# An encoder's forward pass on one core: the SBUF buffers placed in another order, the large ones at multiples of 512 bytes

## The reference

```python
def reference(x, mem, diff_w_qkv, ..., ctx_2, ada_w_2, ssd_w_in_2, ..., ffn_w_out_2):
    x = first_block(x, mem, ...)       # differential attention, dilated attention;
                                       # after each: cross-attention to mem, conv GLU network
    return second_block(x, c_2, ctx_2, ...)   # adaptive norms; an SSD mixer (context, then
                                              # latent), a conformer convolution, two SwiGLU

def memory_cross_attention(x, mem, w_q, w_kv, w_o):
    q = (x @ w_q).reshape(B, S, H, E)
    kv = (mem @ w_kv).reshape(B, M, 2, H, E)
    s = jnp.einsum('bshe,bmhe->bhsm', q, kv[:, :, 0]) * (E ** -0.5)
    o = jnp.einsum('bhsm,bmhe->bshe', softmax(s), kv[:, :, 1])
    return o.reshape(B, S, D) @ w_o

def swiglu(h, w_in, w_out):
    u = h @ w_in
    return (jax.nn.silu(u[..., :FFN_HIDDEN]) * u[..., FFN_HIDDEN:]) @ w_out
```

## Time and profile before

| | us |
|---|---|
| median of 3 runs | 2053.28 |
| lowest, highest | 2052.96, 2055.01 |
| the profiled execution | 2055.43 |
| its span, first to last instruction | 2053.7 |

### The profile page before, as it was taken

The page is one execution under the profiler, slowest core; times in us unless marked ns, Lnnn a source line. Parts: engine busy times, 40 slices in busy tenths (PEclk is TensorE's granted clock), DMA queues, the critical chain, the costliest instruction groups (busy, mean ns, idle before and its releaser), DMA issues.

```text
span 2053.7 us, 34088 instructions
## 1 busy us (share of the span) xinstructions
PE 1920.8 (94%) x13629; PEld 1700.4 (83%) x13629; DVE 1109.8 (54%) x1524; ACT 998.6 (49%) x1726; POOL 1252.0 (61%) x585
## 2 busy tenths in 40 slices
PE   7989999999999989989999899898789999999997
PEld 7879799887999866868888788876579988968996
DVE  5472346623700172146667655678728962847981
ACT  4654345543444373435543444377845545525542
POOL 8768467686888405456778344300369886417995
PEclk9999999999999999999999899999999999999999
DMA  7435377774555405357764122211245554324552
GB/s 259 144 129 203 120 269 308 303 264 167 185 186 185 143 1 183 146 218 299 313 257 146 64 81 86 99 64 62 82 154 184 184 185 147 120 82 159 195 187 104
DMA packets 49217, 342.30 MB, mean 167 GB/s; under 512 B 5264, under 2 KB 7312, under 8 KB 8144
## 3 DMA queue, kind: packets, MB, share of 16 engines
q1 hardware_dynamic: 47440, 331.02, 44.1%
q0 software_dynamic: 1664, 9.70, 1.2%
HBM read 339.65 MB, written 1.05 MB: 166 GB/s over the span
## 4 chain that ended last, share of the span: by engine, by line
PE 77%; DVE 11%; ACT 6%; POOL 3%; issue 2%; DMA 1%; DVEq 0%; SPq 0%; ACTq 0%; POOLq 0%
PE bank L1708 13%; PE bank L1712 13%; PE bank L1763 13%; PE bank L1710 12%; PE bank L1813 3%; PE bank L1743 2%; PE bank L1742 2%; PE bank L1740 2%; PE bank L1939 2%; PE bank L1309 2%; PE bank L1311 2%; PE bank L1312 2%; ACT arena L1140 2%; DVE arena L723 2%; PE bank L1531 1%
## 5 line engine op out<-in xcount | busy, mean ns | idle before, releaser
L2219 POOL TENSOR_TENSOR w_lo<-ring,w_hi 128x1024 fp32r<-128x1024 f32 x360 | 877.0, 2465 | 275.2 <-ACT w_hi L2827 258.0
L1708 PE MATMUL bank<-x_hi,w_hi 128*128 128x256 f32 x2176 | 618.5, 284 | 18.6 <-POOL w_lo L2219 14.1
L1712 PE MATMUL bank<-x_lo,w_hi 128*128 128x256 f32 x2176 | 619.7, 285 | 0.0
L2827 ACT ACTIVATE w_hi<-ring 128x1024 fp32r<-128x1024 f32 x448 | 448.9, 1052 | 332.8 <-DMA ring<-slabs_dram 326.1
L1708 PEld LDWEIGHTS bank<-x_hi,w_hi 128*128 128x128 f32 x2176 | 415.8, 191 | 38.5 <-issue 37.3
L1712 PEld LDWEIGHTS bank<-x_lo,w_hi 128*128 128x128 f32 x2176 | 415.0, 191 | 0.0
L1710 PE MATMUL bank<-x_hi,w_lo 128*128 128x256 f32 x1472 | 414.3, 281 | 0.0
L1710 PEld LDWEIGHTS bank<-x_hi,w_lo 128*128 128x128 f32 x1472 | 282.4, 192 | 0.0
L2219 POOL TENSOR_TENSOR w_hi<-ring,w_hi 128x1024 fp32r<-128x1024 f32 x88 | 208.8, 2394 | 102.7 <-ACT w_hi L2827 102.7
L2751 ACT ACTIVATE arena<-bank 128x512 f32<-128x512 f32 (+1 forms) x178 | 97.9, 563 | 279.6 <-PE bank L1712 192.1
L1710 PE MATMUL bank<-x_hi,w_hi 128*128 128x256 f32 x704 | 197.5, 281 | 0.0
(11 more groups left out here) (355 smaller groups left out, 3665.1 us busy)
## 6 DMA issues: line engine op xcount, KB each, us to landing
ring<-slabs_dram SPq DMA_DIRECT2D x308, 1024.0 KB, 4.8
lnrow<-ln_dram POOLq DMA_DIRECT2D x6, 1024.0 KB, 5.3
arena<-slabs_dram SPq DMA_DIRECT2D x4, 1024.0 KB, 8.3
xt<-xT_dram SPq DMA_DIRECT2D x1, 1024.0 KB, 5.9
xt<-memT_dram SPq DMA_DIRECT2D x1, 1024.0 KB, 12.0
x<-x_dram SPq DMA_DIRECT2D x1, 1024.0 KB, 13.6
arena<-ctx_dram POOLq DMA_DIRECT2D x1, 1024.0 KB, 8.0
lnrow<-ln_dram POOLq DMA_DIRECT2D x2, 512.0 KB, 5.0
```

The lines of the kernel that those rows point to most:

```text
L1708: ins = pe.matmul(dst, wh[:, k, c], src[0][:, k, :], start=(k == 0), stop=False)
L1712: ins = pe.matmul(dst, wh[:, k, c], src[1][:, k, :], start=False, stop=(k == KC - 1))
L2219: pool.tensor_tensor(dst[:, c], ring[:, s, c], w_hi[:, s, c].bitcast(F32), ALU.subtract).then_inc(S["lo_ready"], 1)
L2827: a.activation(w_hi[:, g % RING, c], ring[:, g % RING, c], ACT.Copy) \
```

## The change

Only the order of the allocations changes. `row` and `mod` (2176 and 768 bytes) go to the front; `pt`, `small` and `sc_in` (3264, 2304 and 1024 bytes) go behind the arena. All instructions, their order and their waits stay; their SBUF addresses are others.

```diff
+        row = sb("row", [P, NROW])
+        mod = sb("mod", [P, 2, 6, 8, 2])
         ring_at = aligned()
         ring = sb("ring", [P, RING, SLAB])
         x = sb("x", [P, NT, D])
...
         tri_at = aligned()
         tri = sb("tri", [P, 4, NT, T])
         lnrow = sb("lnrow", [P, 2, D])
-        pt = sb("pt", [P, NPT])
-        row = sb("row", [P, NROW])
-        small = sb("small", [P, 576])
-        mod = sb("mod", [P, 2, 6, 8, 2])
-        sc_in = sb("sc_in", [P, KC, 32])
         xlat = sb("xlat", [P, KC, T])
         arena_at = aligned()
         arena = sb("arena", [P, 28672])
+        pt = sb("pt", [P, NPT])
+        small = sb("small", [P, 576])
+        sc_in = sb("sc_in", [P, KC, 32])
```

## The result

| | before | after |
|---|---|---|
| median, us | 2053.57 (4 runs) | 2068.86 (4 runs) |
| lowest, highest | 2052.96, 2055.01 | 2066.51, 2069.48 |
| span of the profiled execution | 2053.7 | 2067.8 |

The changed kernel is slower by 15.3 us between the medians (0.74%); the ratio on record, from the single runs, is 1.0069, 95% interval 1.0056 to 1.0081. The forecast was 2080.8 us, with a range that began at 2070.0.

What follows compares the result with a forecast made beforehand. The prediction took PE's rate between matmul starts as the bound. Its terms summed to 29.4 us, 28.0 at the granted clock, +27.5 after 0.5 off, so 2053.3 + 27.5 = 2080.8 us, range 2070 to 2088.

Steps and rivals of the forecast that it cites:

- What bounds the kernel: Whole span: PE is busy 94%, waits offer little, so only PE's rate from one matmul to the next matters.
- The 256-column terms: x columns rise to 360 ns a triple, 19.6 us; conv networks, m columns and L1740 on m, 6.4 us.
- Half clock: All PE terms: at 1.2 GHz, 4.6% of the time, places cost nothing, so 29.4 us becomes 28.0.
- The 512-column term: L1763 and L1531: two more equal pairs in each group of six matmuls, 3.4 us slower; L1309 unchanged.
- last sign: If PE's spacing is as forecast but the span isn't 20 us longer, something assumed on the path was not.
- Rival B: Faster, about 2020 us: buffers off a 512-byte mark cost, so at 0 every pair gets the cheapest price; 4%.
- Plain fp32: fp32 matmuls such as L1813 run at half the rate and don't depend on places: 0 us.
- Transfers at 0: DMA into the ring lands at 0 instead of 128: taken as 0 us, with -5.5 to +4.3 considered.
- Rival A: Nothing changes, 2053.3 us: PE's two streams don't disturb each other and the levels come from something else; 7%.
- Rival C: Half the effect, 2067 to 2070 us: only pairs equal in more than the low nine bits cost fully; 2%.
- Rival D: Over 2088 us: triples with every pair equal at 0 also meet GpSimd's and ScalarE's reads there; 3%.
- A count of pairs: fp32r triples: each pair of moving operand and next weights at equal addresses modulo 512 costs 6.7 ns.

Runs made afterwards that it cites:

- tri alone: Against the kernel before: only tri (x_lo) and lnrow at 128 modulo 512, every other large buffer at 448; 2052.54 us, ratio 0.9988.
- both at 128: Against the kernel before: xlat and the arena moved to 128 modulo 512, where the ring and its neighbours already began; 2066.89 us, ratio 1.0068.
- ring alone: Against the kernel before: only the ring (w_lo) at 128 modulo 512, everything else large at 448; 2064.48 us, ratio 1.0051.
- 32, 96 and 128 bytes of distance: Three layouts against the kernel before: ring group at 128, arena and xlat at 160, 480 or 0 modulo 512; 2059.74, 2074.74 and 2057.0 us.
- x_hi apart: Against the kernel before: tri at 128, other large buffers at 448 modulo 512, x_hi and x_lo exchanged so x_hi lies in tri; 2059.63 us, ratio 1.0025.
- the ring at 0 and the arena at 448: Against the kernel before: ring and its neighbours moved to 0 modulo 512, xlat and the arena staying at 448; 2059.25 us, ratio 1.0024.
- x_hi apart and the others at 320: Against the kernel before: x_hi in tri at 128, row moved behind the arena, other large buffers at 320 modulo 512; 2060.0 us, ratio 1.0025.

## Why the prediction was wrong in size, point by point

**What bounds the kernel: right.** PE's busy time and the span grew by 14.9 and 14.1 us, its longest wait by nothing. The granted clock is unchanged. In the stretch of the earlier trace rows PE is now never idle, and GpSimd is 12.5 us below it, where it was 10.0 below before (busy us of PE, its loads, VectorE, ScalarE, GpSimd; clock, DMA share):

```profile
1545.00:1665.00 120.00, 120.00 (x1002) 120.00 (x1002) 103.43 (x60) 59.33 (x83) 107.49 (x44) 1.00 0.49 179
```

**The 256-column terms: right.** Forecast 360.0 ns for every form, measured 359.5 to 360.0. The terms of 19.6 and 6.4 us came to 25.4 together, by the table. The rule that gave them, 6.7 ns for each equal pair, is not right: it fails in six of the layouts above. What carried the terms is its upper end, which was measured at 360 (L1740 on x, L1309). That these mixed-place forms have in the mean the same 360 as a form with everything at one place is luck as far as these runs tell; at 512 columns the same step from one to the other failed.

**Half clock: right.** The prediction left the share of time at 1.2 GHz out. At half clock a triple of x columns takes 640 ns before and after, which is one column a cycle (3.2 us over five triples, and 3.9 over six to the tenth of a us, 640 by the starts to the ns; first the kernel before, then the changed one):

```profile
L1708 PE MATMUL bank<-x_hi,w_hi x6: 415/415/416, 501.2 to 504.4; 128*128 128x256 f32 x6
...
L1708 PE MATMUL bank<-x_hi,w_hi x7: 415/415/415, 505.0 to 508.9; 128*128 128x256 f32 x7
```

**The 512-column term: the step that failed.** The prediction priced L1763 and L1531 at two more pairs a group, +3.4 us, and L1309 with 512 columns at 0, because at L1309 "all equal" took 233.3 ns. In fact all of them fell, to 226.7 ns a matmul (L1531 to 228): -10.0 us. That is 13.4 us below the forecast's term, 12.8 at the granted clock, and the gap between the forecast's +27.5 and the span's +14.1 is 13.4. The prediction's own last sign, that with PE's spacing as forecast a small rise would mean something off the path, doesn't apply: the spacing at 512 columns wasn't as forecast.

The wrong reading is in the row that I took as the end of the scale. In L1309 all *pairs* are equal, each moving operand with the weights loaded beside it. But the moving operands themselves change place from one matmul to the next, s_hi at 448 and s_lo at 128, and so do the weights. No 512-column row of the kernel before shows a form whose operands all stand at one place, and I used the nearest as if it did. Its 256-column twin did give the right price, 360.0, which made the reading look safe. But that was a mean. In the kernel before, the two forms that I had at 360 got there by unlike steps: L1740 on x goes 350, 370, 350, 370 ns from triple to triple (352 and 368 unrounded), in order of time:

```profile
561.11 0.28 PE L1740 MATMUL bank<-w_hi,x_hi 128*128 128x256 f32 x1
561.46 0.28 PE L1740 MATMUL bank<-w_hi,x_hi 128*128 128x256 f32 x1
561.83 0.28 PE L1740 MATMUL bank<-w_hi,x_hi 128*128 128x256 f32 x1
562.18 0.28 PE L1740 MATMUL bank<-w_hi,x_hi 128*128 128x256 f32 x1
562.55 0.28 PE L1740 MATMUL bank<-w_hi,x_hi 128*128 128x256 f32 x1
```

Inside a triple of L1309 the starts were 110, 130 and 120 ns apart, in order of time of the kernel before:

```profile
1314.30 0.28 PE L1309 MATMUL bank<-s_hi,w_half 128*128 128x256 f32 x1
1314.41 0.29 PE L1311 MATMUL bank<-s_lo,w_half 128*128 128x256 f32 x1
1314.54 0.29 PE L1312 MATMUL bank<-s_hi,w_lo 128*128 128x256 f32 x1
1314.66 0.28 PE L1309 MATMUL bank<-s_hi,w_half 128*128 128x256 f32 x1
```

In the changed kernel nearly every step is 120. It is another regime with the same mean at 256 columns and another one at 512, and the uneven steps could have warned me. With tri alone, where L1309 reads one place only, the triple falls to 680. In these rows a form with one place takes a fixed time over its columns: 120.0 ns x 2.4 = 288 cycles for 256, 226.7 x 2.4 = 544 for 512, 32 more each time. With mixed places the extra isn't fixed: at 512 columns the kernel before takes 43 to 48 more (231.1 to 233.3 ns), at 256 columns 21 to 32.

I also hadn't written that end into the range. Rival B held that a place could make the 512 columns cheap, but for a wrong reason, the multiple of 512, and together with cheaper 256 columns, so its time was 2020 and not 2068. A fall at 512 beside a rise at 256 was no case of mine, and the low end of 2070 allowed only for a part of the rise being hidden, or for L1763 without effect.

**Plain fp32: right.** L1813 of the changed kernel in order of time: 22 matmuls in 9.61 us, of which the last lasts 0.59, (9.61 - 0.59) / 21 = 429.5 ns each, beside (2.74 - 0.59) / 5 = 430 from the earlier trace rows.

```profile
1836.77 9.61 PE L1813 MATMUL bank<-ring,arena 128*128 128x512 f32 x22
```

The 0.59 us are those of the line's shortest and median row (min/median/max ns):

```profile
L1813 PE MATMUL bank<-ring,arena x50: 592/592/1191, 1826.0 to 1849.6; 128*128 128x512 f32 x50
```

**Transfers at 0: right for the sum, but there is an effect.** On the chain of the changed kernel stand two transfers, where the earlier trace rows is one of four:

```profile
1.53 7.16 DMA ring<-slabs_dram
...
886.54 4.67 DMA ring<-slabs_dram
```

The first load is 0.5 us shorter than the 7.64 us before, and this follows the place. In the three kernels with the ring at 0 it takes 7.14 to 7.27 us, in the nine with the ring at 64, 128 or 192 modulo 256 it takes 7.42 to 7.65. The first 128 packets of 8 KB of the program take exactly 309 ns each in the three, and 321 to 322 in the mean in the nine, 4% more. The Trainium skill, "DMA: Bandwidth & Descriptors", section "How a descriptor splits into AXI transactions", gives a descriptor off a 256-byte boundary an extra transaction; the trace agrees in direction here, and one in 33, the prediction's estimate from that section, is near the 4%. Over the whole program it is lost: the median packet takes 309 ns in every kernel, all 40,064 of them together 14.30 ms before and 14.31 after. The layout with both at 128 takes 2066.89 us, its ratio nearly that of the change. So the effect on the time is the 0.3 to 0.5 us of the first load.

**Rival A: out.** The levels moved with the places in every layout, with the same instructions in the same order. The Trainium skill, "SBUF — State Buffer", section "Who interferes with whom", says that only the port pair of VectorE and GpSimd causes contention and that PE never waits on anyone. It may well wait for no other engine, but its own spacing in these fp32r matmuls goes from 346.7 to 363.2 ns a triple with the places of its operands alone; the measurement decides. **Rival B: out** as it was put, since 128 gives what 0 gives. **Rival C**, pairs equal in more than nine bits: out, since eight bits are enough (0 and 256). Its time of 2067 to 2070 holds the result, by chance: its mechanism has the x columns at 353.4, and they are at 360. **Rival D: out.** No form is above the 360 ns that equal pairs alone give, and the time is 12 us below the forecast, not above 2088.

**What stays open.** Why 64 bytes apart costs 346.7 in one layout and 353.3 in another, and why 96 apart costs more than equality. A count of pairs told the 256-column levels right in the kernel before, in the changed one and with tri or the ring alone, and failed with the ring at 0, with 32, 96 and 128 bytes of distance, and with x_hi apart. In the two with one stranger and 353.3 to 353.4, one of PE's two streams stays at one place while the other changes; in the kernel before both change. That both change isn't enough, as the ring at 0 shows, where both do and the level is 353.3. Where two layouts agree modulo 256 in all that a form reads, its level agrees too, though the buffers lie thousands of bytes further or nearer: 353.6 and 353.5 for the conv networks (before, tri alone), 353.4 twice for the m columns and 2773 twice for L1763 on h (before, ring alone). The x columns with unequal places were never repeated in that way, so for them it isn't shown that the place modulo 256 is all that counts. Nor do the levels give the whole time of a layout: with the ring at 0 and the arena at 448 the steady steps add 9.3 us, and the span is 4.9 us longer. No run here looks inside PE.

## What to carry to other kernels

When PE is the bound, read the distance between starts form by form, and note for each where the moving operand and the stationary one begin modulo 256: here the places alone were worth from -0.1% to +1.0% of the time, and alignment as such was worth half a microsecond at most, in the first load. Before pricing a change with "the row where everything is equal", check that in that row everything is equal that the change makes equal, the successive operands too, and in both sizes: the same edit cost 13.3 ns a triple at 256 columns and gave 20 at 512. A rule fitted to the levels of one layout is a forecast for another only where it has been seen to hold in a third.

## What the runs showed of the hardware that I had not expected

- With every operand at one place modulo 256, the next fp32r matmul starts 32 cycles later than its columns would ask, at 256 columns (120.0 ns) and at 512 (226.7 ns). That is the dearest but one at 256 and the cheapest at 512.
- 256 bytes apart is the same place (2068.93 us), 96 apart is worse than the same for the x columns (2074.74 us, 363.2 ns a triple).
- At half clock the places don't count: 640 ns a triple before and after.
- An 8 KB packet that lands off a 256-byte boundary took 321 to 322 ns in the mean and not 309, in the program's first load; later it doesn't show.
- A mean can hide two steps that take turns: 351 and 362 ns with x_hi apart and the others at 320, 352 and 368 for L1740 on x in the kernel before. With all operands at one place nearly every step is 120 ns.
- VectorE's busy time fell by 24.7 us in the changed kernel, and by 36 with both at 128, with its instructions unchanged. The groups by line show where (busy us, mean ns of one; the two rows are of the changed kernel): L2432 took 96.9 us, 2202 ns each, before, and takes 1157 ns each now, while L2434 went from 1077 to 1932. It is off the path. The traces show two lengths for these operations, about 425 and about 2420 ns. Of L2432's 44, 4 were short before and 27 are now; of L2434's, 27 were and 12 are. The long ones of the two lines lie beside GpSimd's subtractions of L2219 for 92 to 100% of their time, the short ones for 28 to 31%. So they meet GpSimd's at other moments now. That PE's pace moves them apart is not tested, and the operands of these operations changed their places too.

```profile
L2434 DVE TENSOR_TENSOR h_lo<-arena,h_hi 128x256 f32 x40 | 77.3, 1932 | 4.9
L2432 DVE TENSOR_TENSOR arena<-arena 128x256 f32<-128x256 f32 x44 | 50.9, 1157 | 29.1 <-ACT arena L2899 20.2 <-DVE h_lo L2434 6.4
```
